# Expert sums four pairs behind the dots, and nearly all of the third tile's sums on VectorE

## What is computed

```
q = (x @ w_q).reshape(n_tok, PEER_HEADS, 2, PEER_KEY_DIM // 2)
s = jnp.einsum('thpd,hpnd->thpn', q, subkeys)
half_s, half_i = lax.top_k(s, PEER_TOPK)
...
def expert_block(args):
    xt, e, g = args
    act = gelu(jnp.einsum('td,tkd->tk', xt, jnp.take(u_tab, e, axis=0))) * g
    return jnp.einsum('tk,tkd->td', act, jnp.take(v_tab, e, axis=0))
```

## Time and profile before

| | |
|---|---|
| median of 3 runs | 3575.6 us (3564.45 to 3580.89) |
| the profiled execution | 3569.56 us |
| its span, first to last instruction | 3567.7 us |
| PE busy | 2629.8 us (74%) |
| DVE busy | 2088.4 us (59%) |
| POOL busy | 1710.3 us (48%) |
| ACT busy | 677.3 us (19%) |
| HBM read | 1065.67 MB, 300 GB/s over the span |

### The profile page before, as it was taken

One profiled execution on the slowest core, in us unless ns is written; L12 is line 12 of the kernel. 1 busy time (PEld: TensorE's weight loads), 2 busy tenths in 40 slices (PEclk: granted clock), 3 DMA queues, 4 the chain that ended last, 5 costly groups with the idle time before them and its releaser, 6 DMA issues. The chain is left out here.

```text
span 3567.7 us, 29649 instructions
## 1 busy us (share of the span) xinstructions
PE 2629.8 (74%) x8956; PEld 1513.1 (42%) x8956; DVE 2088.4 (59%) x5138; ACT 677.3 (19%) x1797; POOL 1710.3 (48%) x1540
## 2 busy tenths in 40 slices
PE   6889974568778878568688786655877878676666
PEld 1467753222345544224355563522344545232222
DVE  2453336964675564963455645599555656965555
ACT  0022200111023211111133411111133311111111
POOL 0000001645565654663354433257574766777776
PEclk9789987779889999789889897877988989788888
DMA  5432324879999999897677675679998999999998
GB/s 201 177 124 89 112 106 159 325 272 394 394 411 357 356 380 389 311 323 280 226 272 267 236 290 218 253 274 365 349 416 354 385 418 418 347 348 381 362 366 301
DMA packets 262812, 1070.99 MB, mean 300 GB/s; under 512 B 29824, under 2 KB 30592, under 8 KB 233728
## 3 DMA queue, kind: packets, MB, share of 16 engines
q0 software_dynamic: 221184, 805.40, 59.8%
q1 hardware_dynamic: 38304, 253.14, 18.3%
q10 hardware_dynamic: 3168, 10.55, 0.7%
HBM read 1065.67 MB, written 3.31 MB: 300 GB/s over the span
## 5 line engine op out<-in xcount | busy, mean ns | idle before, releaser
L631 PE MATMUL psum<-ring,wdiag 128*128 128x512 f32 x1732 | 947.6, 694 | 459.1 <-ACT wdiag L925 445.8
L1589 POOL DMA_INDIRECT ring<-in_peer_u,experts x418 | 470.2, 1125 | 1087.5 <-DVE experts L1386 630.8
L1589 POOL DMA_INDIRECT ring<-in_peer_v,experts x583 | 642.5, 1102 | 491.0 <-PE psum L631 323.7
L631 PEld LDWEIGHTS psum<-ring,wdiag 128*128 128x128 f32 x1732 | 366.7, 222 | 943.9 <-issue 907.1
L1589 POOL DMA_INDIRECT work<-in_peer_u,experts x350 | 395.8, 1131 | 162.9 <-issue 98.4
L1164 DVE SCALAR_TENSOR_TENSOR acc<-ring,wts,acc 128x1024 f32<-128x1024 f32 x144 | 185.0, 1285 | 407.8 <-issue 364.4
L719 PE MATMUL psum<-work,wring 128*128 128x128 f32 (+1 forms) x2048 | 367.5, 339 | 43.5 <-DMA wring<-in_wpack 35.3
L719 PEld LDWEIGHTS psum<-work,wring 128*128 128x128 f32 x2048 | 328.5, 201 | 98.0 <-issue 59.3
L631 PE MATMUL psum<-work,wdiag 128*128 128x512 f32 x500 | 275.7, 695 | 84.8 <-ACT wdiag L925 81.8
L1140 DVE CUSTOM_DVE_ANT_0 work<-work 128x1024 f32<-128x1024 f32 x280 | 333.7, 1221 | 6.7 <-DMA work<-in_peer_u,experts 3.8
L707 PE MATMUL psum<-wring,work 128*128 128x512 f32 (+1 forms) x672 | 301.3, 609 | 21.1 <-DMA wring<-in_wpack 14.7
(11 more groups left out here) (181 smaller groups left out, 2638.4 us busy)
## 6 DMA issues: line engine op xcount, KB each, us to landing
wring<-in_wpack SPq DMA_DIRECT2D x220, 1024.0 KB, 7.8
wring<-in_wpack SPq DMA_DIRECT2D x24, 512.0 KB, 7.4
ring<-in_peer_v,experts POOLq DMA_INDIRECT x583, 6.4
ring<-in_peer_u,experts POOLq DMA_INDIRECT x418, 6.4
work<-in_peer_u,experts POOLq DMA_INDIRECT x350, 6.5
work<-in_rows ACTq DMA_DIRECT2D x4, 1024.0 KB, 10.5
wring<-in_wpack SPq DMA_DIRECT2D x4, 896.0 KB, 10.0
work<-in_peer_v,experts POOLq DMA_INDIRECT x185, 6.5
```

Of the source, the lines that this page charges most:

```text
L631: last = nc.tensor.matmul(psum[:, 6 + q, :], wdiag[:, SUM_NO[e] % SMALL, :], row(V_SLOT[e])[:, 512 * q:512 * (q + 1)], start=(e % KSEL == ...
L1589: pool.indirect_dma_start(row(slot), None, a[table], index).then_inc(got[slot], 16)
```

## The change

```diff
-SHARE = [4, 4, 2, 4, 4, 4]
+SHARE = [4, 4, 1, 4, 4, 4]

 def by_vector(e):
     k, every = e % KSEL, SHARE[e // KSEL]
-    return k >= 8 and k % every == every - 1
+    return k >= 2 * LAG_SUM and k % every == every - 1
...
                 def expert_step(g):
+                    p = g - LAG_SUM
+                    if 0 <= p < ALL_STEPS:
+                        for e in range(PAIR * p, PAIR * (p + 1)):
+                            if by_vector(e):
+                                add_row(e)
                     if g < ALL_STEPS:
...
                         if e >= SMALL:
                             dve.wait_ge(diags_made, sums_before(e - SMALL + PAIR, False))
+                        if e >= SMALL and sums_before(e - SMALL + PAIR, True):
+                            dve.wait_ge(rows_acc, sums_before(e - SMALL + PAIR, True))
                         nc.vector.tensor_tensor(wts[:, s:s + PAIR], acts[:, s:s + PAIR], gates[:, tk:tk + PAIR], ALU.mult).then_inc(wts_ready, 1)
-                        for e in range(PAIR * p, PAIR * (p + 1)):
-                            if by_vector(e):
-                                add_row(e)
```

## The result

The changed kernel took 3449.4 us in the median (3442.67 to 3452.73, 4 runs), the kernel before beside it 3570.0 us: a ratio of 0.9657, 95% interval 0.9625 to 0.9689, or 121 us less where 88 were forecast. The sum it rests on doesn't add up the way it was written: tile 2 gave less than forecast, the other tiles seven times as much.

A forecast was written before the change was run, and what follows sets the result against it. DMA engines were taken to bound all tiles but tile 2, where engines wait for one another, VectorE for v blocks. 20 + 60 + 20 - 20 + 8 = 88 us off 3575.6 gave 3488 us, range 3400 to 3570.

The forecast's parts named there:

- The 187 us of waits for v go, and u is late next: Tile 2: VectorE's sums no longer wait 187 us for v blocks; u blocks in the 4-slot ring are late next.
- Projections 20 us: Tile 2, 1622 to 1747 us: eight sums fewer on PE and no v wait before the norms, 20 us gained.
- The last stretch 20: Tile 2, from 2125 us to the search at 2297 (output, norm, queries): 20 us gained, bounds 0 and 48.
- Step 192 and its next minus 20: Step 192 and the next three: asks queue behind VectorE's sums, dots come late, 20 us lost, bounds 0 and 30.
- The middle 60: Tile 2's mixing, 1775 to 2125 us: DMA engines become the floor at share 0.92, 60 us gained, bounds 0 and 84.
- The other tiles 8, tile 5 at most 7 us: Outside tile 2: DMA shares near 1 leave little, 8 us gained, upper end 50; tile 5 at most 7.
- The sign I had named: Tile 5: waits for v that only turn into waits for u would confirm that nothing comes from there.
- The asks' price: Tile 2: asks starting beside a dot take 1.68 us, not 0.94; up to 44 us more of GpSimd, counted as nothing.
- Rival 2, the clock: Mixing's middle: without the sums TensorE's granted clock falls to 0.73, costing some 35 us of the gain: 3523 us, chance 0.11.
- Rival 3, other waits: Tile 2: waits for u blocks or PE's results replace those for v; middle gives 15, last stretch 5: 3548 us, chance 0.17.
- Rival 4: Slower: in tile 2 waits for v become nearly equal waits for u while added sums cost VectorE; 3623 us, chance 0.08.

The follow-up runs named there:

- e8: The kernel before with every v block asked for two experts earlier (V_LAG 4 for 6), nothing else: 3472.2 us, 0.9734.
- e4: The changed kernel with the last eight sums of tile 2 back on TensorE: 3430.1 us, 0.9615.
- e1: The changed kernel with the split as before (60 of tile 2's sums on VectorE), VectorE's sums still four pairs behind: 3430.8 us, 0.9598.
- e9: The changed kernel with TensorE also making the 60 sums of tile 2 that went to VectorE, counted twice in the output: 3457.7 us, 0.9673.
- e10: The changed kernel with the 60 sums of tile 2 that left TensorE made by VectorE over 8 of their 1024 columns: 3412.8 us, 0.9551.
- e3: e1 with only tile 2's sums four pairs behind, the other tiles' two behind at the end of the step: 3490.8 us, 0.9779.

## Why the prediction was right, and where it wasn't

- *The 187 us of waits for v go, and u is late next.* Right in tile 2: 7.8 us are left, and dots wait 20.1 us where they had waited 0.4. e8 shows that the order of the asks makes the wait.
- *Projections 20 us:* 18.3. *The last stretch 20:* 23.2. *Step 192 and its next minus 20:* minus 17.4, by the mechanism named, and e4 takes it away. *The middle 60:* 39.0. The term was mis-sized because I took 0.92 of the DMA engines as what paces it afterwards; the share reached only 0.79. By e1, e4, e9 and e10 the later place alone gives 49, PE's relief 0 to 11, and VectorE's load takes 15 to 26. VectorE's 42 us should have been put on the path by about half. Tile 2 in all gave 63 of the 80; it lasted 683 us for 746 with a DMA share of 0.73, where the prediction looked for 650 to 670 and 0.78.
- *The other tiles 8, tile 5 at most 7 us:* wrong, and the step that failed. They gave 58. I read a DMA share of 0.98 as full. It was the share at which GpSimd's asks came, 1.116 + 0.30 us each; the rate went to 405 GB/s once they were shorter. The sign I had named came and misled: in tile 5 the waits for v did turn into waits for u (162.1 to 7.0, and 5.2 to 131.4 us), and the tile still lasted 22 us less. So 121 us against 88 is the right size from a sum with two large errors, 17 too much in tile 2 and 50 too little elsewhere.
- *The asks' price, "I count nothing":* the row with the 1.68 us was the right one to look at, and I weighed it only where asks have slack, in tile 2, and only as a cost of more sums. In tile 5 they have no slack, and after the change fewer of them began inside a dot or sum (16, not 51), by where VectorE's operations fell and not by more gaps.
- *Rival 2, the clock:* its mechanism came true in part, 0.82 against 0.91 before and 0.95 in e1, inside a stage that still got faster. *Rival 3, other waits:* in part. In steps 132 to 195 VectorE's idle time was 337 us, 199 of it for v; after, it was 200 us, with 9 for v, 25 for u and 166 for others, where others had been 136. Of the 191 us of waits that went, then, 74 were filled by the added sums, 53 by waits for u and others, and 63 shortened the stretch. *Rival 4:* in tile 2 u's waits came to a tenth of v's, so it didn't.
- *Two moves as one change.* I costed the later place and the split as one sum. Apart, the place is worth 137 us (e1, 3567.95 to 3430.8), and the split costs some 20 beside it. By the profiles of e1 and the changed kernel that is 14 us in the search and steps 192 to 195 (91.2 for 76.8) and 10 in the middle, less 6 in the projections; tile 5's 11 us the other way are of the same program in both.
- Open: the 14 us of tiles 0 and 1 and the 22 of tiles 3 and 4 come with the later place (e3), but there the asks are not shorter (in steps 196 to 319 541.98 us for 496 before, 545.47 for 489 after), so it is not tile 5's mechanism. What fell is the time in which GpSimd asks for nothing, from 275 to 250 us in those steps and from 427 to 396 in steps 0 to 131; in steps 196 to 319 its waits for dots fell from 67 to 51 us and for TensorE's sums from 71 to 64. Slots come free earlier against its asks, then. No run took it apart.

## What to carry to other kernels

Where one queue brings the operands of several consumers in order, look at which operand each consumer needs and how far behind the others it was asked for; a consumer that stands one place too early waits for the newest ask each time, and one number, either the distance of the asks or of the consumer, may be worth more than moving its work to another engine. A DMA share near 1 doesn't say that the DMA engines are the limit: divide the stretch by the number of issues and see whether the issuing engine ran without a gap. Where its issues can be held by another engine's operations, look at where in those operations they begin; waits that go need not shorten anything there. And an unload of one engine onto another should be costed at every point where the new maker's place in its own order gates somebody's slot.

## What the runs showed of the hardware that I had not expected

- GpSimd's issue of an indirect gather takes 0.94 us. One that begins inside a two-input operation of VectorE (1.22 to 1.28 us) is held and ends 0.81 us after that operation ends, so it takes 1.96 to 1.98 us at most; between operations it keeps 0.94, and VectorE's own operation is not lengthened. In tile 5 this alone moved the mean ask from 1.116 to 0.989 us and the rate from 370 to 405 GB/s.
- The DMA share was 0.98 at 370 GB/s and 1.02 at 405: it rose by 4% where the rate rose by 9%.
- PE's granted clock in the middle of the mixing was 0.95 with 33 sums of PE in 321 us, 0.90 with them in 370 us, and 0.86 without them in 310 us.
